# Two-branch encoder layer in f32 on one core: gate decays through DRAM, and gate-row transposes inside the projections of tiles 3 and 4

## The reference, cut to what matters

```
xn = rmsnorm(x, pre_g);  proj = xn @ w_in            # 1024 x 10256 columns, split into 10 parts
gates = proj[m_g] + gate_b                           # 16 columns: i_fw, f_fw, i_bw, f_bw, for 4 heads
log_f = log_sigmoid(f)
# per head, forward and on the flipped sequence, chunk by chunk:
a = cumsum(log_f in the chunk);  b = i - a
m_new = max(A + m, max(A - a + i))                   # A: a at the chunk's end; m: running stabiliser
w_k   = exp(A - a + i - m_new)                       # per token
decay = exp(A + m - m_new)                           # one number per chunk, head and direction
C = decay * C + sum(w_k * k v^T);   n = decay * n + sum(w_k * k)
h = (w_inter * (q C) + s v) / max(|w_inter * (q n) + sum s|, exp(-m_j))
```

## Time and profile before

| what | value |
|---|---|
| median of 3 runs | 1620.06 us (1619.62 to 1621.73) |
| the profiled execution, its own time | 1619.34 us |
| its span (first to last instruction) | 1617.6 us |
| TensorE matmul busy | 1575.8 us |
| VectorE, ScalarE, POOL busy | 914.8, 816.6, 489.9 us |
| mean granted TensorE clock, as a share of full speed | 0.991 |
| share of TensorE in the chain that ended last | 84% |

### The profile page before, as it was taken

The page is one execution under the profiler, slowest core; times in us unless marked ns, Lnnn a source line. Parts: engine busy times, 40 slices in busy tenths (PEclk is TensorE's granted clock), DMA queues, the critical chain, the costliest instruction groups (busy, mean ns, idle before and its releaser), DMA issues.

```text
span 1617.6 us, 24048 instructions
## 1 busy us (share of the span) xinstructions
PE 1575.8 (97%) x8567; PEld 1316.3 (81%) x8567; DVE 914.8 (57%) x1548; ACT 816.6 (50%) x1458; POOL 489.9 (30%) x595
## 2 busy tenths in 40 slices
PE   6999999999999999999999999999999998999998
PEld 5788888888888877788878887888888887888998
DVE  6803774774775637777676767676764112434413
ACT  5314554664655635555555555555554324555312
POOL 4242142251152142222222222222221333433650
PEclk8999999999999999999999999999999999999999
DMA  5131121031121131111111111111111535333422
GB/s 168 31 127 39 27 86 46 26 91 39 56 73 40 32 85 31 40 40 43 39 49 29 43 39 50 28 43 39 49 59 51 195 104 177 126 99 98 127 88 105
DMA packets 138254, 111.50 MB, mean 69 GB/s; under 512 B 5995, under 2 KB 125740, under 8 KB 138165
## 3 DMA queue, kind: packets, MB, share of 16 engines
q1 hardware_dynamic: 133556, 97.74, 20.5%
q10 hardware_dynamic: 4608, 12.58, 2.0%
HBM read 85.10 MB, written 21.00 MB: 66 GB/s over the span
## 4 chain that ended last, share of the span: by engine, by line
PE 84%; DVE 6%; ACT 5%; issue 3%; POOL 1%; DMA 1%; SPq 0%; DVEq 0%; ACTq 0%; POOLq 0%
PE ps L750 57%; PE ps L758 7%; PE ps L951 6%; PE ps L1058 6%; PE ps L964 3%; DVE state_f L1349 1%; ACT num L1819 1%; PE ps L839 1%; PE ps L991 1%; PE ps L777 1%; DVE h_sum L1376 1%; ACT sigmoid_work L1632 1%; PE ps L973 1%; ACT kw_split L1799 1%; DVE num L1328 1%
## 5 line engine op out<-in xcount | busy, mean ns | idle before, releaser
L750 PE MATMUL ps<-xn_split,w_split 128*128 128x512 f32 x4224 | 1024.3, 398 | 0.4 <-DVE gate_cols L1254 0.4
L750 PEld LDWEIGHTS ps<-xn_split,w_split 128*128 128x128 f32 x4224 | 785.2, 189 | 181.5 <-issue 16.7
L630 POOL TENSOR_TENSOR w_split<-w_raw,w_split 128x256 fp32r<-128x256 f32 x384 | 318.6, 861 | 976.4 <-ACT w_split L1617 976.2
L1903 ACT ACTIVATE probs<-ps,negmax 128x1024 f32<-128x1024 f32 x128 | 142.7, 1115 | 104.7 <-DVE negmax L1438 103.5
L1463 DVE TENSOR_TENSOR aT_split<-ps,aT_split 128x512 fp32r<-128x512 f32 x128 | 88.3, 689 | 133.9 <-ACT aT_split L1908 133.9
L1438 DVE TENSOR_REDUCE negmax<-ps 128x1 f32<-128x1024 f32 x128 | 150.7, 1219 | 16.9 <-PE ps L951 16.9
L1908 ACT ACTIVATE aT_split<-ps 128x512 fp32r<-128x512 f32 x128 | 76.5, 598 | 103.1 <-PE ps L964 103.0
L951 PE MATMUL ps<-ak_split,aq_split 64*128 64x512 f32 x768 | 106.2, 408 | 3.0 <-DVE ak_split L1394 3.0
L758 PEld LDWEIGHTS ps<-aT_split,va_split 128*128 128x128 f32 x768 | 95.8, 189 | 5.3 <-issue 3.4
L1617 ACT ACTIVATE w_split<-w_raw 128x1024 fp32r<-128x1024 f32 x94 | 98.9, 1053 | 0.0
L758 PE MATMUL ps<-aT_split,va_split 128*128 128x256 f32 x768 | 97.9, 284 | 0.4
(11 more groups left out here) (238 smaller groups left out, 1649.8 us busy)
## 6 DMA issues: line engine op xcount, KB each, us to landing
w_raw<-in_w_in SPq DMA_DIRECT2D x80, 512.0 KB, 3.9
qk_f<-spill_g SPq DMA_DIRECT2D x16, 512.0 KB, 3.5
spill_g<-qk_f ACTq DMA_DIRECT2D x12, 512.0 KB, 2.6
w_argument<-m_rows SPq DMA_DIRECT2D x8, 512.0 KB, 5.2
spill_m<-hT_f ACTq DMA_DIRECT2D x16, 256.0 KB, 2.1
spill_a<-o_out SPq DMA_DIRECT2D x32, 128.0 KB, 1.8
h_split<-spill_m SPq DMA_DIRECT2D x8, 512.0 KB, 4.9
w_raw<-in_w_branch_m SPq DMA_DIRECT2D x8, 512.0 KB, 5.8
```

The source lines that it names most:

```text
L630: lo = pool.tensor_tensor(wsp[b][:, 1, ks_], raw[b][:, ks_], wsp[b][:, 0, ks_].bitcast(F32), ALU.subtract)
L750: mm = pe.matmul(ps[:, half, :], wsp[b][:, wl, k, :], moving[:, xl, k, cols], start=(k == 0 and n == 0), stop=(k == KT - 1 and n == 2))
L1903: act.activation(pr[:, c], ps[:, 2 + 2 * c:4 + 2 * c, :].rearrange("p b k -> p (b k)"), ACT.Exp, bias=nmax[:, b, c:c + 1], accum_out=den[: ...
```

## The change

The decays no longer go through TensorE. SyncE waits for the exponential of `decay`, stores the 2 x 4 x 8 numbers in a DRAM tensor `d_rows`, and after the m rows are stored and their broadcasts issued it waits for that store and reads the numbers back into all 128 partitions, one load for each head. VectorE waits for these loads before the loop over the heads. The matrix `pick`, its copy, its 16 matmuls and the copy `decay_all` are gone.

The 32 transposes are split into four blocks of 8, one each in the middle of the four halves of tiles 3 and 4. The reversing product moves from behind tile 6 to between tiles 5 and 6, and waits for `col_rev`.

```diff
@@ SyncE, after the load of tile 7 @@
+            sp.wait_ge(prep_act, prep_act_at("decay"))
+            for r in range(2):
+                sp.dma_start(d_rows[r], r_dec[32 * r:32 * r + MH, :]).then_inc(d_rows_stored, 16)
             sp.wait_ge(prep_dve, prep_dve_at("m_rev"))
             sp.dma_start(m_rows[0], r_m[0:MH, :]).then_inc(m_rows_stored, 16)
             sp.dma_start(m_rows[1], r_reset[32:32 + MH, :]).then_inc(m_rows_stored, 16)
             sp.wait_ge(m_rows_stored, 16 * 2)
             load_w_arg(0)
+            sp.wait_ge(d_rows_stored, 16 * 2)
+            for m in range(MH):
+                sp.dma_start(decay[:, m].rearrange("p (r c) -> p r c", r=2), d_rows[:, m].partition_broadcast(P)) \
+                    .then_inc(decay_loaded, 16)
@@ TensorE @@
             proj_half(0, 0, 0, 0, 1)
-            for j in range(1, 6):
+            for j in range(1, 3):
                 proj_half(0, 0, 0, j, 0)
                 proj_half(0, 0, 0, j, 1)
 
-            pe.wait_ge(prep_act, prep_act_at("decay"))
-            for m in range(MH):
-                for r in range(2):
-                    at = 256 + 2 * NC * m + NC * r
-                    mm = pe.matmul(ps[:, 7, at:at + NC], pick[:, r, m, :], r_dec[:], start=True, stop=True)
-            mm.then_inc(prep_pe, 1)
-
-            pe.wait_ge(prep_act, prep_act_at("w_k"))
-            for q, row in enumerate((r_i, r_winter, r_t, r_wk)):
+            def gate_columns(q):
+                pe.wait_ge(prep_act, prep_act_at("w_k"))
+                row = (r_i, r_winter, r_t, r_wk)[q]
                 for c in range(NC):
                     mm = pe.transpose(ps[:, 2 + q, c * ROWS:(c + 1) * ROWS], row[:, c * P:(c + 1) * P],
                                       ident[0:ROWS, 0:ROWS])
-            mm.then_inc(prep_pe, 1)
+                if q == 3:
+                    mm.then_inc(prep_pe, 1)
+
+            for j in range(3, 5):
+                proj_half(0, 0, 0, j, 0, amid=lambda: gate_columns(2 * j - 6))
+                proj_half(0, 0, 0, j, 1, amid=lambda: gate_columns(2 * j - 5))
+            for half in range(2):
+                proj_half(0, 0, 0, 5, half)
+            pe.wait_ge(prep_dve, prep_dve_at("col_rev"))
+            pe.matmul(ps[:, 7, 0:NC * Q_ALL * MH], rev[:], colrev[:].rearrange("p c q m -> p (c q m)"),
+                      start=True, stop=True).then_inc(prep_pe, 1)
             for half in range(2):
                 proj_half(0, 0, 0, 6, half)
-
-            pe.wait_ge(prep_dve, prep_dve_at("decay_all"))
-            pe.matmul(ps[:, 7, 0:NC * Q_ALL * MH], rev[:], colrev[:].rearrange("p c q m -> p (c q m)"),
-                      start=True, stop=True).then_inc(prep_pe, 1)
@@ VectorE @@
-            mark(dve.tensor_copy(pick[:], ident[0:ROWS, 0:64].rearrange("p (r x) -> p r x", r=2)[:, :, 0:MH].unsqueeze(3)
-                                 .to_broadcast([ROWS, 2, MH, P])), "pick")
...
-            dve.wait_ge(prep_pe, 4)
+            dve.wait_ge(prep_pe, 3)
...
-            mark(dve.tensor_copy(decay[:], ps[:, 7, 256:256 + 16 * MH].rearrange("p (m c) -> p m c", m=MH)), "decay_all")
-            dve.wait_ge(prep_pe, 5)
+            dve.wait_ge(prep_pe, 4)
...
+            dve.wait_ge(decay_loaded, 16 * MH)
             with dve.Fori(0, MH - 1) as h:
```

More of the change, by code:

```diff
@@ L73 @@
 V_BM, V_AG, V_ROWS = V_MG + KT, V_MG + 3 * KT, V_MG + 3 * KT + 1
-PREP_DVE = ("wg_zero", "wg_hi", "wg_lo", "vecs", "conv0", "again", "bmerge", "pick",
+PREP_DVE = ("wg_zero", "wg_hi", "wg_lo", "vecs", "conv0", "again", "bmerge",
             "lam_products", "lam_sums", "i_fw", "i_bw", "f_fw", "f_bw", "abs_f", "log_f", "a", "b",
             "carry", "max", "m_prev", "decay", "w_inter", "a_plus_m", "w_k", "m_rev",
-            "neglam", "col_fw", "col_rev", "decay_all", "col_bw")
+            "neglam", "col_fw", "col_rev", "col_bw")
 PREP_ACT = ("lam_exp", "exp_f", "ln_f", "decay", "w_inter", "emj", "w_k")
@@ L145, in hybrid_block @@
         spill_a = nc.dram_tensor("spill_a", [KT, P, S], F32, kind="Internal").ap()
+        d_rows = nc.dram_tensor("d_rows", [2, MH, NC], F32, kind="Internal").ap()
         m_rows = nc.dram_tensor("m_rows", [2, MH, S], F32, kind="Internal").ap()
@@ L215, in hybrid_block @@
         r_wk, r_winter = r_f, r_carry
-        pick = sb("pick", [ROWS, 2, MH, P], at=p_scope)
         rev = sb("rev", [P, P], at=p_scope)
@@ L292, in hybrid_block @@
         m_rows_stored = sem("m_rows_stored")
+        d_rows_stored = sem("d_rows_stored")
+        decay_loaded = sem("decay_loaded")
         w_arg_loaded = sem("w_arg_loaded")
```

## The result

The changed kernel takes 1624.39 us, the median of 20 runs (1622.61 to 1626.19), against 1621.44 for the kernel before on the same chip (20 runs, 1617.51 to 1625.97). The ratio is 1.0018, with a 95% interval from 1.0011 to 1.0025: 3 us slower, where 4 us faster was forecast. The profiled execution has a span of 1621.8 us against 1617.6.

The account below looks back on a forecast made before the run. TensorE, busy for 97% of the span, was taken to bound the kernel. -1.88 - 1.77 - 0.64 = -4.29 from 1619.34 gave 1615.0 profiled; keeping the timed runs' 0.7 us distance gave 1615.8 us, range 1613.4 to 1619.0.

Parts of the forecast that it names:

- Picks gone, -1.88: Before tile 6, the 16 picking matmuls leave TensorE's chain, saving 1.88 us.
- Half clock behind them, -1.77: Tile 6's 48 matmuls run at full clock, 11.0 us in place of 12.79, saving 1.77 us.
- Reversing product, -0.64: Moved between tiles 5 and 6, it spares TensorE a 0.37 us wait and a 0.27 us start from rest.
- Transposes moved, 0: Four blocks of 8 inside tiles 3 and 4 still take 2.02 us, costing nothing extra; upper bound 1.1 us.
- Decays by DMA, VectorE, POOL, 0: Before head 0, added stores and loads, VectorE's lost copies and POOL's later split stay hidden, costing 0 us.
- Beyond this stage TensorE is the chain in nearly every piece, so the 4.3 us should be carried to the end: After the edited stage, TensorE bounds nearly everything, so the whole 4.3 us gain lasts to the kernel's end.
- Rival 1: A half-clock stretch appears or goes in mLSTM heads 0 to 3: one more 1617.3, upward 0.20; one fewer 1614.2, downward 0.14.
- Rival 2: Tile 6's half-clock stretch is absent from timed runs before, or stays after: -2.5, 1617.5 us; chance 0.08.
- Rivals 3 to 5: Transposes bring half-clock stretches, 1622.9 (0.05); decay loads land late at head 0, 1625 (0.03); late column copies, at most 0.64 back.

Follow-up runs that it names:

- experiment 3: Kernel before with the transposes in four blocks and the reversing product ahead of tile 6, picking products kept after tile 5: 1621.10 us, ratio 1.0012.
- experiment 6: Changed kernel, and kernel before with decays by DMA alone, each with 64 waits where TensorE waits for input anyway: 1618.04 us, 0.9972; 1617.58 us, 0.9974.
- experiment 1: Changed kernel with 64 waits on a long-set semaphore ahead of TensorE's first product: 1618.35 us against 1620.30, ratio 0.9987.

## Why the prediction was wrong, step by step

- *Picks gone, -1.88:* right. *Half clock behind them, -1.77:* right in the changed kernel, and experiment 3 puts it down to the picks. (12.79 less 11.0 is 1.79; the slip changes nothing.) *Reversing product, -0.64:* right, 60 matmuls follow it in 13.74 us.
- *Transposes moved, 0:* mis-sized. Each block cost 0.12 us more itself and 0.21 us in the matmuls around it, 1.3 us in all and beyond my bound of 1.1. I had taken it from the input's transposes, which read 128 rows as the projections do; these read 36. In the trace their first weight load no longer begins under the running matmul: TensorE's loader is idle for 0.36 us ahead of each block. That the height of the tile is the reason was only argued. With this term the sum is -3.0, which is what the stage gained.
- *Decays by DMA, VectorE, POOL, 0:* right, nothing of TensorE waited for them.
- *"Beyond this stage TensorE is the chain in nearly every piece, so the 4.3 us should be carried to the end":* this is the step that failed. The 3.0 us did reach the attention (it begins 3.3 us earlier), but the edit also moved all later code of TensorE, and the two turns of its attention loop gave back 8.1 us. I had counted the edit's time and not its instructions. The kernel before shows the sign in its waits by engine, the one large wait of its TensorE that no work explains (us in total, times, longest), and I did not ask what stood there:

```profile
PE ps L964 <- issue: 3.7, 2, 1.9
```

  With the loop in its old place the change is worth 1621.93 x 0.0028 = 4.5 us (2.9 to 6.2 by the interval) in experiment 6, which holds the forecast's 4.3 and the trace's 3.0 alike, and 2.1 us (0.6 to 3.4) in experiment 1, which holds the 3.0 alone. The place alone is then worth 5.0 to 7.5 us, from 0.9987 or 0.9972 to 1.0018.
- *Rival 1* was right in kind: which of the heads 0 to 3 had a half-clock stretch varied from trace to trace, from none to three of them (1 and 2 before, 1 and 3 in the changed kernel). It was not what turned the sign. *Rival 2* did not hold where it could be seen: both traces with picks have the stretch; what timed runs have is not known. The mean granted clock of the timed runs was 0.9897 for the change, 0.9911 for the kernel before beside experiment 6, and 0.9926 for the change with late waits; for the decays by DMA alone it was 0.9885, and 0.9922 with late waits. The second stall costs clock besides its own length. *Rivals 3 to 5* did not come.
- None of the rivals for "slower" was the real one. It needed no late data, only 32 instructions fewer.

## What to carry to other kernels

Before an edit to a kernel with long hardware loops, look for "issue" stalls of the bounding engine at the loops' turns, and count by how many instructions the edit moves the loops; a gain of 0.3% can be turned into a loss by that alone. Measure an edit at two or three code places, with idle waits as padding where the engine stands anyway, before it is judged. Small products that keep TensorE busy but do little work cost their own time and may bring half-clock time behind them; few large groups of 36-row transposes were cheaper than many small ones.

## What had not been expected of the hardware

- A turn of the attention loop, of 1968 TensorE instructions, costs 1.5 to 2.1 us of standing, and 2.8 to 5.0 us when the loop begins 2 to 18 instructions ahead of the place found here. Its second pass fetched 9 blocks of instructions before and 10 in the changed kernel. The mLSTM loop, of 1254 instructions, shows no such stall at its turns, and the instruction queue moved nothing from 235 to 490 us, while that loop turned twice.
- Wherever a turn had a second stall (1.2 to 2.5 us, or the joint one), a stretch of 3.4 or 6.8 us at 1.2 GHz began close to it, from 1.1 us ahead of it to 0.8 us behind its end. With one stall alone there was none at a turn in the traces with four blocks or with none, but one at one turn in each of the three one-block traces.
- 64 waits on a semaphore that is long set become 32 instructions of TensorE. What they cost in time was not settled: the gate products ended between 47.7 and 49.0 us in the traces with waits (mean 48.4), and between 47.2 and 48.2 in those without (mean 47.7).
